# Feed-forward entries computed on x times the norm's weights, with the norm's factor and the shift applied behind PSUM

## What is computed

```
y = x * rsqrt(mean(x*x) + 1e-6) * g          # norm over the 1024 features
h = y * (1 + scale) + shift                  # scale, shift, gate come from the condition
a, u = split(h @ wi, 2)                      # 1024 -> 2 * 2816
x = x + 0.5 * gate * ((silu(a) * u) @ wo)    # 2816 -> 1024
```

## Time and profile before

| | us |
|---|---|
| median of 3 runs | 3235.24 (3233.91 to 3236.9) |
| the profiled execution | 3234.64 |
| its span, first to last instruction | 3232.1 |
| PE busy | 3152.3 (98%) |
| DVE busy | 1860.3 (58%) |
| ACT busy | 1026.0 (32%) |
| mean granted clock of TensorE | 0.986 of full |

### The profile page before, as it was taken

The page is one execution under the profiler, slowest core; times in us unless marked ns, Lnnn a source line. Parts: engine busy times, 40 slices in busy tenths (PEclk is TensorE's granted clock), DMA queues, the critical chain, the costliest instruction groups (busy, mean ns, idle before and its releaser), DMA issues.

```text
span 3232.1 us, 37291 instructions
## 1 busy us (share of the span) xinstructions
PE 3152.3 (98%) x15190; PEld 2528.8 (78%) x15190; DVE 1860.3 (58%) x2673; ACT 1026.0 (32%) x1480; POOL 10.2 (0%) x23
## 2 busy tenths in 40 slices
PE   8999999998899999999999999999999998899998
PEld 7888888776678888788877888788887764578887
DVE  7876555645555554666646554566665655554444
ACT  4212222345442222322234222332224344332222
POOL 0000000000000000000000000000000000000000
PEclk9999999999999999999999999999999999899999
DMA  6433432210034433255522443235551210123331
GB/s 229 140 118 124 149 125 85 66 44 11 1 124 152 154 124 117 85 207 190 197 92 79 169 144 131 79 118 206 190 178 62 76 55 1 56 91 102 97 98 52
DMA packets 101846, 365.03 MB, mean 113 GB/s; under 512 B 11247, under 2 KB 12543, under 8 KB 101421
## 3 DMA queue, kind: packets, MB, share of 16 engines
q1 hardware_dynamic: 100636, 357.94, 32.4%
q0 software_dynamic: 1040, 4.71, 0.4%
HBM read 360.51 MB, written 2.10 MB: 112 GB/s over the span
## 4 chain that ended last, share of the span: by engine, by line
PE 89%; DVE 6%; ACT 3%; issue 1%; DMA 1%; SPq 0%; POOL 0%; DVEq 0%; ACTq 0%; POOLq 0%
PE ps L192 25%; PE ps L194 25%; PE ps L193 25%; PE ps L196 4%; PE ps L197 2%; DVE SQ L610 1%; PE ps L496 1%; DVE HL L599 1%; DVE WL L184 1%; PE ps L2373 1%; ACT WH L179 1%; PE ps L2606 0%; DVE XT L855 0%; DVE RAW L1317 0%; PE ps L2706 0%
## 5 line engine op out<-in xcount | busy, mean ns | idle before, releaser
L192 PE MATMUL ps<-HH,WH 128*128 128x512 f32 x2464 | 973.8, 395 | 4.2 <-ACT S L769 2.2
L194 PE MATMUL ps<-HH,WL 128*128 128x512 f32 x2464 | 960.9, 390 | 0.0
L193 PE MATMUL ps<-HL,WH 128*128 128x512 f32 x2464 | 960.0, 390 | 0.0
L179 ACT ACTIVATE WH<-RAW 128x1024 fp32r<-128x1024 f32 x456 | 459.1, 1047 | 622.4 <-PE ps L194 366.5
L184 DVE TENSOR_TENSOR WL<-RAW,WH 128x1024 fp32r<-128x1024 f32 x456 | 542.9, 1219 | 92.3 <-ACT WH L179 92.1
L192 PEld LDWEIGHTS ps<-HH,WH 128*128 128x128 f32 x2464 | 462.9, 188 | 116.7 <-issue 9.9
L194 PEld LDWEIGHTS ps<-HH,WL 128*128 128x128 f32 x2464 | 462.7, 188 | 98.7
L193 PEld LDWEIGHTS ps<-HL,WH 128*128 128x128 f32 x2464 | 463.1, 188 | 97.1 <-issue 4.6
L855 DVE SCALAR_TENSOR_TENSOR XT<-ps,DER,XT 128x512 f32<-128x512 f32 x512 | 346.4, 682 | 249.0 <-PE ps L194 234.2
L192 PE MATMUL ps<-GH,WH 128*128 128x512 f32 x1056 | 412.5, 391 | 4.8 <-DVE GL L793 4.8
L194 PE MATMUL ps<-GH,WL 128*128 128x512 f32 x1056 | 411.1, 389 | 0.0
(11 more groups left out here) (356 smaller groups left out, 2467.8 us busy)
## 6 DMA issues: line engine op xcount, KB each, us to landing
RAW<-in_w_modt SPq DMA_DIRECT2D x200, 512.0 KB, 5.0
RAW<-in_ffn_wi SPq DMA_DIRECT2D x176, 512.0 KB, 4.8
RAW<-in_ffn_wo SPq DMA_DIRECT2D x88, 512.0 KB, 4.9
RAW<-in_w_gu SPq DMA_DIRECT2D x88, 512.0 KB, 4.3
RAW<-in_w_in SPq DMA_DIRECT2D x44, 512.0 KB, 3.6
RAW<-in_w_down SPq DMA_DIRECT2D x44, 512.0 KB, 4.2
RAW<-in_w_out SPq DMA_DIRECT2D x16, 512.0 KB, 4.4
STG<-in_w_modt SPq DMA_DIRECT2D x10, 512.0 KB, 12.8
```

The costliest lines, as they stand in the source:

```text
L179: act.e.activation(u.hi, u.ld.view, ACT.Copy).then_inc(u.hi_done.sem, 1)
L192: pe.e.matmul(out, wh, x[0], start=first, stop=False)
L193: pe.e.matmul(out, wh, x[1], start=False, stop=False)
L194: m = pe.e.matmul(out, wl, x[0], start=False, stop=last)
```

## The change

Five entries change: mi = 2, 3, 5, 6 and 8. Chunk 0 (at mi = 6, behind the double norm, chunks 0 and 1) is multiplied with x times the weight, `UH`/`UL`, and not with the normed input. The factor of the norm (per token) multiplies the result behind PSUM, and the shift, carried through the weights to one number per inner feature (`BIAS`), is added there. The other chunks use the normed input as before.

- `AheadSplit(k-1)` makes `UH` and `UL` of slice k-1. It stands behind the step that evacuates slice k, in the last Down, the output products and the pooling mixer. In the output products the loop is rewritten, and the banks of the eight steps go from `d % 3` to (0, 1, 2, 4, 5, 6, 4, 5).
- All eight slices of squares are added on DVE (`SumsEnd`). `Factor` sums over the partitions and spreads in one matmul with a full matrix of ones (128x512), issued inside Up 0 behind k = 2 (at the double norm the second inside Up 1 behind k = 5); square root and Newton step work on 128x512. `RstdSum`, `RstdSpread` and `Busy` go at these entries.
- `BiasDot`: two more slabs of weights are loaded, and DVE makes eight dependent operations on 128x256; `BiasSum`: two matmuls of one column; `BiasCopy` on ACT.
- Chunk 1 too (at mi = 6 chunk 2) is computed with k outermost; the two `Spread` products of the modulation stand behind chunks 2 and 3 instead of 0 and 1.

```diff
+class SumsEnd(Step):
+    def vector(self, dve):
+        self.sums.late(dve, 8)
+
+class AheadSplit(Step):
+    def scalar(self, act):
+        act.wait_ge(*self.ready)
+        act.wait_ge(*self.gain)
+        act.e.activation(P.UH[:, k, :], P.XT[:, k, 0:T], ACT.Identity, scale=self.a).then_inc(self.hi.sem, 1)
+    def vector(self, dve):
+        dve.wait_ge(*self.hi)
+        dve.e.scalar_tensor_tensor(P.UL[:, k, :], P.XT[:, k, 0:T], self.a, P.UH[:, k, :].bitcast(F32),
+                                   ALU.mult, ALU.subtract).then_inc(self.lo.sem, 1)
+
+class FactorProd(Step):
+        dve.e.tensor_tensor(self.R, self.R, self.second.R, ALU.mult).then_inc(self.done.sem, 1)
+
+class Factor(Step):
+    def sum(self, pe):
+        pe.wait_ge(*self.total)
+        pe.wait_ge(*self.bankfree)
+        pe.e.matmul(P.banks[7], P.ONE, P.SA[:, 0:T], start=True, stop=True).then_inc(self.summed.sem, 1)
+
+class BiasDot(Step):
+        for k in range(8):
+            w, b = self.view[:, :, k * 128:(k + 1) * 128], P.mod_b(self.mi, k)
+            if k == 0:
+                dve.e.tensor_scalar(P.ACC, w, b, None, ALU.mult).then_inc(self.part[k].sem, 1)
+            else:
+                dve.wait_ge(*self.part[k - 1])
+                dve.e.scalar_tensor_tensor(P.ACC, w, b, P.ACC, ALU.mult, ALU.add).then_inc(self.part[k].sem, 1)
 class Up(Step):
-        if self.c == 0:
+        if self.mixed:
             for n in range(len(F.segs)):
                 for k in range(8):
                     for q in range(2):
                         products(q, n, k)
+                    if self.factor and k == F.at[self.c]:
+                        self.factor.sum(pe)
+                if q == 0 and self.factor:
+                    act.wait_ge(*self.scaled[q])
+                    act.wait_ge(*self.biased)
+                    act.e.activation(s, s, ACT.Silu, bias=P.BIAS[:, 2 * c + q:2 * c + q + 1]).then_inc(self.silu[n].sem, 1)
+                if self.factor:
+                    dve.e.tensor_tensor(d, out, self.apply.R, ALU.mult).then_inc(self.scaled[q].sem, 1)
+                    if q:
+                        dve.wait_ge(*self.silu[n])
+                        dve.e.scalar_tensor_tensor(s, d, P.BIAS[:, 2 * self.c + q:2 * self.c + q + 1], s, ALU.add, ALU.mult).then_inc(self.mul[n].sem, 1)
+                        dve.wait_ge(*self.hi[n])
+                        dve.e.tensor_tensor(gl, s, gh.bitcast(F32), ALU.subtract).then_inc(self.lo[n].sem, 1)
 def ffn
+            if ahead:
+                units, self.units = self.units, self.split([wi[1], wi[NF + 1]])
+                F.factor[0] = F.apply = self.add(Factor(self, R))
+                if final:
+                    over = Sums(self, T, True)
+                    self.add(FinalNorm(self, final, over, R))
+                    self.add(SumsEnd(over))
+                    second, third = self.units, self.split([wi[2], wi[NF + 2]])
+                    F.factor[1] = self.add(Factor(self, R2))
+                    F.apply = self.add(FactorProd(self, F.factor[0], F.factor[1]))
+                    self.add(Up(F, 0, units))
+                    self.add(NormSplit(self, mi, segs, F.h, after, R=R2))
+                    self.add(Up(F, 1, second))
+                    self.units = third
+                else:
+                    self.add(NormSplit(self, mi, segs, F.h, after, R=R))
+                    self.add(Up(F, 0, units))
                     for d in range(8):
                         self.add(DownPart(down, d))
+                        if nxt is not None and last and d:
+                            self.add(AheadSplit(self, nxt, d - 1, down.evac[d - 1, 0][0], bias.get("gains")))
                         if d in (1, 3, 5):
                             split_ahead()
+                    if nxt is not None and last:
+                        self.add(SumsEnd(sums))
+                        self.add(AheadSplit(self, nxt, 7, down.evac[7, 0][0], bias.get("gains")))
 def out_products
+                if d:
+                    self.add(AheadSplit(self, nxt, d - 1, evac[d - 1]))
+                if d == 1:
+                    bias["lds"] = self.bias_loads(wi)
+                elif d == 2:
+                    bias["dot"] = self.add(BiasDot(self, nxt, bias["lds"]))
+                elif d == 4:
+                    self.add(BiasSum(bias["dot"]))
+                elif d == 5:
+                    self.add(BiasCopy(bias["dot"]))
+                elif d == 7:
+                    self.add(SumsEnd(sums))
+                    self.add(AheadSplit(self, nxt, 7, evac[7]))
+        for d in range(8):
+            ahead = self.split([w[d + 1]]) if d < 7 else None
+            if d in (5, 6):
+                later += self.split([following[d - 5]])
+            job(d)[1](units)
 def mixer_pool
+                    adds[k] = self.add(PoolAdd(self, mi, means[g], o, bfree, sums))
+                    if k:
+                        self.add(AheadSplit(self, mi + 1, k - 1, adds[k - 1].evac))
-            self.add(Busy(self, 4))
```

More of the change, by code:

```diff
@@ new lines, with __init__, vector @@
+class BiasDot(Step):
+    def __init__(self, P, mi, lds, chunk=0):
+        self.P, self.mi, self.lds, self.chunk = P, mi, lds, chunk
+        self.accfree = P.accfree
+        self.before, self.shift = P.biased, P.modt[mi, 0]
+        self.part = [P.s["bias_dve"].next() for _ in range(8)]
+        self.summed = P.accfree = P.s["bias_mm"].next()
+        for ld in lds:
+            ld.users = [self.part[7]]
+        at = [ld.slot for ld in lds]
+        lo, step = min(at), abs(at[0] - at[1])
+        self.view = P.RAW[:, lo:lo + step + 1:step, :]
+        self.order = [at.index(lo), 1 - at.index(lo)]
+    def vector(self, dve):
+        P = self.P
+        for ld in self.lds:
+            dve.wait_ge(*ld.landed)
+        dve.wait_ge(*self.accfree)
+        dve.wait_ge(*self.before)
+        dve.wait_ge(*self.shift)
+        for k in range(8):
[5 more added lines that the diff above has]
+                dve.e.scalar_tensor_tensor(P.ACC, w, b, P.ACC, ALU.mult, ALU.add).then_inc(self.part[k].sem, 1)
@@ new lines, with __init__, tensor @@
+class BiasSum(Step):
+    def __init__(self, dot, bank=7):
+        self.dot, self.bank, self.col = dot, bank, 508 + 2 * dot.chunk
+    def tensor(self, pe):
+        P, dot = self.dot.P, self.dot
+        pe.wait_ge(*dot.part[7])
+        for i, q in enumerate(dot.order):
+            m = pe.e.matmul(P.banks[self.bank][:, self.col + q:self.col + q + 1], P.ACC[:, i, :], P.ONE[:, 0:1], start=True, stop=True,
+                            skip_group_check=True)
+        m.then_inc(dot.summed.sem, 1)
@@ L654, with __init__, scalar @@
+class BiasCopy(Step):
+    def __init__(self, dot, bank=7):
+        self.dot, self.bank = dot, bank
+        dot.P.biased = self.done = dot.P.s["bias_act"].next()
+    def scalar(self, act):
+        P = self.dot.P
+        act.wait_ge(*self.dot.summed)
+        c = 2 * self.dot.chunk
+        act.e.activation(P.BIAS[:, c:c + 2], P.banks[self.bank][:, 508 + c:510 + c], ACT.Copy).then_inc(self.done.sem, 1)
 class Ffn:
@@ L690, in __init__ @@
                 self.free[q, n] = F.ufree[b]
[L691 removed]
+        self.mixed = c <= len(F.factor)
+        order = [(q, n) for n in range(ns) for q in range(2)] if self.mixed else [(q, n) for q in range(2) for n in range(ns)]
         for at in order:
@@ L3043, in norm_split, with bias_loads, ffn @@
         return h
-    def ffn(self, mi, segs, wi, wo, after, following, blk=None, rows=(), early=()):
+    def bias_loads(self, w, c=0):
+        return [self.add(LoadStep(Load(self, src))).ld for src in (w[c], w[NF + c])]
+    def ffn(self, mi, segs, wi, wo, after, following, blk=None, rows=(), early=(), ahead=False, nxt=None, dot=None, final=None):
         with self.scope() as ctx:
```

181 lines of the change are left out of this document (145 added, 36 removed).

## The result

| | before | changed |
|---|---|---|
| median, us | 3235.37 (3233.91 to 3236.9, 4 runs) | 3256.78 (3254.47 to 3259.5, 4 runs) |
| ratio | | 1.0066, 95% interval 1.0049 to 1.0084 |
| profiled execution, span, us | 3234.64, 3232.1 | 3259.5, 3257.0 |
| mean granted clock | 0.986 | 0.977 |

What follows compares the result with a forecast made beforehand. PE was taken as the bound, losing about 9.1 us per entry. Entry, stall and BiasSum terms of 5.8 us plus 11.2 for the clock gave 17.0 on 3234.64, 3251.6, so a median of 3252; range 3226 to 3262.

Steps and rivals of the forecast that it cites:

- The hand-over chain: Last Down before entries 3 and 6: chained ACT and DVE operations take 2.73 us per slice against PE's 2.04.
- Rival 1: Last Down: hand-over does not bind, evacuations keep 2.04 us; 25 us less than forecast, 3227; chance 0.18.
- Entries 2 and 8: Behind output products: gains of 4.4 and 5.2 us, less 2.7 each for BiasDot's stall before step 4.
- table load: Behind the norm at the entries: silu's 1.28 us load taken as hidden, done before, costing nothing.
- rival 4: Chunk 0: PE waits in it instead of in front, also at entries 2 and 8; +8, 3260; 0.13 with rival 3.
- The wait before chunk 2: At entries: chunk 2's weight split queues behind chunk 0's evacuation; start at norm end + 5.8 us, 5.0 at entry 8.
- TensorE's clock: Behind seven bare PE waits of 2.7 us and more: half clock costs 1.6 us each, +11.2 in all.
- Rival 2: Behind the new PE waits: the clock does not fall; 3239 us, within the bound of no change; chance 0.10.
- rival 3: Behind the new waits: clock falls longer, or table switches cost the skill page's figure; up to 3264; 0.13 with rival 4.
- Entry 3: Behind the last Down: late sum of squares and later chunk 2, at 1340.8 instead of 1336.5; +4.3 us.
- Entry 5: Behind the pool: six evacuations turn at 2.73 instead of 1.26; chunk 2 at 1746.2 instead of 1743.0, +3.2 us.
- Entry 6: Double norm: two chunks pulled forward, their gain taken back by waits of 6.4, 7.3 and 4 us; +0.5 us.

Runs made afterwards that it cites:

- e1: Changed kernel with ACT's high part of slice d-1 ahead of square d in the last Down and the pool; 3232.84 us, ratio 0.9987.
- e4: Changed kernel with a silu on six numbers behind each entry's last root, to load silu's table early; 3245.79 us, ratio 1.0034.
- e7: Changed kernel, high part ahead of square, BiasDot behind step 4's split, chunk 2's weight split ahead of chunk 0's evacuation except at entry 6; 3209.25 us, ratio 0.9915.
- e8: Changed kernel with idle Busy products in the new PE waits (11, 6, 9, 0, 9 at the entries, 6 before each step 4); 3246.21 us, ratio 1.0029.
- e9: The changed kernel itself run once more, nothing edited, its second execution; 3256.21 us, ratio 1.0063 to the kernel before.
- e3: Changed kernel with the weight split of chunk 2 (chunk 3 at entry 6) right behind the norm, ahead of chunk 0's evacuation; 3235.51 us, ratio 1.0001.
- e6: Changed kernel with the new entry only at 2 and 8; entries 3, 5 and 6 as in the kernel before; 3239.33 us, ratio 1.0013.

## Why the prediction was right, step by step

**The hand-over chain (right).** Forecast: 0.78 + 0.54 + 0.75 + 0.66 = 2.73 us per slice. Measured: 2.73. The last evacuation was forecast 8.4 us later (1314.3 for 1305.87); counted from PE's restart it is 23.73 - 15.25 = 8.5 later, and the wait inside chunk 0 is 5.82 where 6.2 stood, at entry 6 5.83 where 6.4 stood. PE's loss at d = 7 was put at 1.9 and is 1.17 (the wait that ends at 1312.63), which changes nothing, as the sum is later. Rival 1 falls with this trace, for its condition was that the evacuations keep 2.04 us. Its price, some 25 us for evacuations about 8.5 us earlier at three entries, is borne out in scale by e1: 17.4 to 19.1 us for 5.9, 4.2 and 6.0.

**Entries 2 and 8 (right but for the table load below).** There is no wait in chunk 0, as the 5.4 us of a step cover the chain, so rival 4 is out. The forecast had chunk 2 26.85 us behind the output product's last matmul T, and 31.2 in the kernel before. T in the changed kernel (timeline of PE):

```profile
941.42 0.39 PE L194 MATMUL ps<-MH,WL 128*128 128x512 f32 x1
```

Chunk 2 starts at 969.56, 28.1 behind it, and at entry 8 27.4 behind it (2875.95 to 2903.30), where 26.05 stood. So the entries gained 3.1 and 3.8 us and not 4.4 and 5.2; the 1.3 missing from each is what e4 gives back there. The stall before step 4 (forecast 2.7, measured 2.60 twice) and the clock then took more than this gain. In e7 the two stretches are 5.2 and 5.0 shorter than before, but there the early split has also shortened the wait before chunk 2.

**The wait before chunk 2 (right in kind, undersized at its end).** Forecast: chunk 2 can start 5.8 us behind the norm. At entry 3 the norm ends at 1341.87 (L603 at 1341.12 + 0.75) and chunk 2 starts at 1349.21, 7.3. Of the missing 1.5 silu's table load is 1.28. This is the term of my sum that failed: I had it at nothing because in the earlier trace rows the load stands in front of the wait. Here it stands behind it, since ACT waits for DVE's scaled values before. The Trainium skill (ScalarE: Activation LUTs, § What ACT_TABLE_LOAD costs) puts a switch at 2.66 us with a drain. The rows differ from it: the load takes 1.28 and the activation starts 0.01 later, and e4 gains 1.3 per entry. So 3258, the time that I gave by the Trainium skill, lies closer to the measured 3256.78 than my forecast, but by luck: the place of the load cost this, at four entries, and not a drain at five. Its 2.66 less 1.28 would also make an estimated 1.4 per entry and not the 1.2 that I used.

**TensorE's clock (right in kind, oversized).** Forecast 11.2, seven waits at 1.6 each. Measured with e8: 7.3 us for six of them. The seventh, 4 us before chunk 3 at entry 6, did not come: chunk 2 there runs at half clock until 2149.9 and takes 13.7 us, PE then waits 0.53 us (2158.54, for DVE's `CC`), and DVE's chain sets the time as forecast. The windows of the changed kernel show why it is less (stretch, length, busy, granted clock):

```profile
917.70:921.10 3.40, 3.40 (x8) 2.72 (x9) 2.49 (x4) 2.19 (x3) 0.00 (x0) 0.50 0.92 336
...
2853.80:2857.20 3.40, 3.40 (x15) 2.81 (x16) 2.49 (x4) 2.20 (x3) 0.00 (x0) 1.00 0.92 346
...
1349.21:1352.61 3.40, 3.40 (x15) 2.83 (x16) 2.39 (x4) 1.72 (x3) 0.00 (x0) 1.00 0.72 177
```

Behind the waits of 2.60 (at 2851) and 2.53 (at 1346) the clock stayed whole, and 15 matmuls started in 3.4 us, where behind the first there were 8. Rival 2 (no fall) is ruled out. Of rival 3 (it falls for longer) one case costs time here: behind the wait at entry 2 the half clock lasted from 968.9 to 975.7 in the first execution and to 972.2 in the second. The Trainium skill (TensorE: Matmul & The Clock Gate, § HAM oscillation — how this bites in real kernels) says that a long wait puts the array back and the next work starts at half rate. By that, the trace agrees for the waits of 3.65 us and more: all seven new ones went with a clock of 0.50 in the work behind them, though four of these falls (the two in chunk 0, the one in the pool and that before chunk 2 at entry 6) were followed by a wait for DVE, so that they cost little or nothing.

**Entry 3.** Forecast +4.3 and 1.6 of clock. In the first execution, without a fall of the clock behind the wait before chunk 2, it is 5.6, that is 4.3 and the table load; in the second, with one, 7.2.

**Entry 5 (undersized).** Forecast +3.2 and 1.6 of clock, measured 7.0 and 6.9. The unforeseen wait of 3.69 in the pool for ACT's `Z` looks like the cause, and is not: DVE's evacuations turn at 2.73 straight through it (1719.08, 1721.80, 1724.52, 1727.25, 1729.97, then 1732.79). Counted from PE's restart in the last Down of mi = 3, the forecast had the last evacuation at 57.9, the sum at 61.4 and chunk 2 at 84.4 us. Measured: 58.2, 61.7 and 85.9. So the chain came as forecast and chunk 2 1.5 later, of which the table load is 1.3. With the clock (1.6, the fall from 1760.8) and one `BiasSum` in a Down that PE paces (0.37) this is 3.2 + 1.5 + 1.6 + 0.4 = 6.7 of the 7.0.

**Small terms.** `BiasSum` in an output product: matmuls start 0.60 us apart over it (924.60 to 925.20) instead of 0.23, 0.37 where 0.5 stood. Of the two in Downs that PE paces, for which 1.0 stood, the trace has one (at 2053.05). Entry 6: forecast +0.5 and 1.6 of clock, measured +0.3 and +0.4, as that fall did not come; the cancellation was real, for e1 alone makes that stretch 7.9 shorter than before.

**The sum.** Forecast 17.0; the edited stretches have 19.1 and 19.4; the medians 21.4 and 20.6. Clock -3.9 (-1.6 for the fall that did not come at entry 6, -2.3 for the others) and table load +5.2 (four entries) bring the sum to 18.3, and `BiasSum`, three times 0.37 for a forecast 2.0, to 17.4; the last 2 us of the stretches are not located. So the two terms that I had most wrong had opposite signs, and that the total came within 5 us owes something to this. What lies between 19 and 21 is in unedited code and stays open.

## What to carry to other kernels

Before an operation is added to two engines that hand a tile back and forth, write down the chain in list order for one slice and compare it with PE's time for that slice: 2.73 us against 2.04 lost, against 5.4 it cost nothing. When an edit moves work out of the path, look at what the queue does right behind it: here the weights of the next chunk, a table load and eight tiny operations stood in front of what PE wanted, and three reorderings turned 21 us of loss into 27 of gain. A new bare wait of PE has a second price in the clock, 7.3 us for six waits here, and can be told from the wait itself by filling it with idle products. And a long wait of PE that a change brings is not yet a cost: the 3.69 us in the pool cost next to nothing, because DVE's chain, and not PE, set the pace there.

## What the hardware showed that was not expected

The same pause does not always have the same consequence. PE's 2.60 us before step 4 of the second output product was followed by a granted clock of 1.00 in the first execution of the changed kernel (the window 2853.80 above) and by 0.50 in the second (e9: timeline of PE, then the window):

```profile
2849.41 0.62 PE L192 MATMUL ps<-MH,WH 128*128 128x512 f32 x1 [2.60 <-DVE WL L184]
```

```profile
2849.60:2853.00 3.40, 3.40 (x9) 2.65 (x9) 2.49 (x4) 2.19 (x3) 0.00 (x0) 0.50 0.93 364
```

In the first output product it was the other way round (0.50 in the first execution, 1.00 in the second). In six executions that leave this pause bare there are twelve pauses of 2.60 or 2.61 us: six were followed by half clock (one each in the two executions of the changed kernel, both in e1 and e4) and six not (both in e3 and e6). That moves a stretch by 1.6 us with no difference in the program, and executions of one kernel here lie up to 10 us apart (e1: 3226.73 to 3236.82). And a table load has no fixed place relative to the wait of its activation: it ran ahead of the scaled values at 1330.44 in e3 and behind them at 1342.54 in the changed kernel, with the same two lines of code for the activation. What decides that was not settled.
